# One decoder layer: all blocks projected first, three attentions and the routings moved beside the expert gathers

## What is computed

```python
h = x + W_o[ groupnorm(MLA heads) | groupnorm(FoX heads) ](rmsnorm(x))
y = h + PEER(rmsnorm(h))
# attention, 16 heads, causal over blocks of 128 queries:
s = q k^T * scale (+ c_q - c_k for the eight FoX heads); p = softmax(s + mask); o = p v
# PEER, per token and head (8 heads):
s = q . sub_keys (two sets of 128); top 16 of each; top 16 of the 256 sums; gate = softmax
act = gelu(peer_u[expert] . xb);  out = sum over 128 experts of (gate * act) * peer_v[expert]
```

## Time and profile before

| | us |
|---|---|
| median of the runs | 2458.63 |
| profiled execution, its own span, first to last instruction | 2563.8 |
| PE busy | 1793.9 (70%) |
| DVE busy | 1169.1 (46%) |
| POOL busy | 1190.8 (46%) |
| ACT busy | 348.5 (14%) |
| moved by DMA | 775.33 MB, mean 302 GB/s |
| first gather of peer_u issued | 513.3 |

### The profile page before, as it was taken

The page is one execution under the profiler, slowest core; times in us unless marked ns, Lnnn a source line. Parts: engine busy times, 40 slices in busy tenths (PEclk is TensorE's granted clock), DMA queues, the critical chain, the costliest instruction groups (busy, mean ns, idle before and its releaser), DMA issues.

```text
span 2563.8 us, 31875 instructions
## 1 busy us (share of the span) xinstructions
PE 1793.9 (70%) x11105; PEld 728.5 (28%) x11105; DVE 1169.1 (46%) x2804; ACT 348.5 (14%) x744; POOL 1190.8 (46%) x1076
## 2 busy tenths in 40 slices
PE   6788788855376999988399987631777523227878
PEld 1446445622232343333133332210111100001212
DVE  2334434499822702655680024765800155561352
ACT  1113213100011121322021212200000000000000
POOL 0000000046613656865665565688655444484673
PEclk9876888977689999999599997855899955557997
DMA  4000006069938999999999998999999999999995
GB/s 193 20 9 18 10 1 247 17 251 384 373 131 313 384 399 390 399 393 379 342 331 397 402 382 287 370 365 404 399 405 405 408 405 404 404 392 377 342 352 215
DMA packets 254251, 775.33 MB, mean 302 GB/s; under 512 B 36513, under 2 KB 45370, under 8 KB 250762
## 3 DMA queue, kind: packets, MB, share of 16 engines
q0 software_dynamic: 150784, 547.43, 55.3%
q1 hardware_dynamic: 102138, 221.64, 23.3%
q10 hardware_dynamic: 1168, 4.23, 0.4%
HBM read 766.36 MB, written 6.81 MB: 302 GB/s over the span
## 4 chain that ended last, share of the span: by engine, by line
PE 44%; DMA 24%; issue 12%; DVE 8%; POOL 5%; another core or an unknown queue 3%; ACT 2%; SPq 1%; DVEq 0%; POOLq 0%; ACTq 0%
DMA arena<-peer_v,idxT 14%; PE ps L1562 9%; PE ps L1624 9%; DMA arena<-peer_u,eidx 8%; PE ps L1368 7%; POOL arena L475 5%; PE ps L1610 3%; PE ps L1491 3%; PE ps L1640 2%; DVE arena L1176 2%; PE ps L1422 2%; DMA arena<-kpe_pool 2%; PE ps L1437 1%; PE ps L1412 1%
## 5 line engine op out<-in xcount | busy, mean ns | idle before, releaser
L475 POOL DMA_INDIRECT arena<-peer_u,eidx x512 | 622.2, 1215 | 872.5 <-DVE eidx L1086 512.8
L475 POOL DMA_INDIRECT arena<-peer_v,idxT x512 | 515.0, 1006 | 452.1 <-PE ps L1562 345.5
L1176 DVE CUSTOM_DVE_ANT_0 arena<-arena 128x1024 f32<-128x1024 f32 x384 | 467.0, 1226 | 529.9 <-DMA arena<-peer_u,eidx 457.7
L1562 PE MATMUL ps<-arena 128*32 128x512 f32 x2048 | 554.4, 632 | 125.9 <-DMA arena<-peer_v,idxT 112.5
L1624 PE MATMUL ps<-arena 128*128 128x512 f32 x512 | 303.4, 676 | 15.8 <-DMA arena<-kpe_pool 13.5
L1694 PE MATMUL ps<-arena 128*32 128x512 f32 x512 | 118.0, 874 | 236.5 <-DMA arena<-vn_pool 236.5
L1562 PEld LDWEIGHTS ps<-arena 128*32 128x32 f32 x2048 | 102.9, 111 | 441.0 <-DMA arena<-peer_v,idxT 321.1
L728 ACT ACTIVATE arena<-ps 128x512 f32<-128x512 f32 x256 | 150.0, 596 | 572.3 <-PE ps L1624 240.0
L1610 PE MATMUL ps<-arena 128*32 128x128 f32 x2048 | 177.1, 286 | 44.6 <-issue 35.6
L1368 PE MATMUL ps<-arena 128*128 128x512 f32 (+3 forms) x400 | 174.4, 597 | 6.9 <-DVE arena L952 6.6
L1176 DVE CUSTOM_DVE_ANT_0 arena<-arena,ps 128x1024 f32<-128x1024 f32 x128 | 151.4, 1219 | 11.4 <-DMA arena<-peer_u,eidx 5.3
(11 more groups left out here) (305 smaller groups left out, 1712.1 us busy)
## 6 DMA issues: line engine op xcount, KB each, us to landing
arena<-kt_pool SPq DMA_DIRECT2D x256, 320.0 KB
arena<-vn_pool SPq DMA_DIRECT2D x256, 320.0 KB
arena<-w_q SPq DMA_DIRECT2D x16, 1024.0 KB, 19.5
arena<-w_in SPq DMA_DIRECT2D x8, 1236.0 KB, 15.9
arena<-w_o SPq DMA_DIRECT2D x16, 512.0 KB, 6.9
arena<-peer_u,eidx POOLq DMA_INDIRECT x512
arena<-peer_v,idxT POOLq DMA_INDIRECT x512
arena<-kpe_pool SPq DMA_DIRECT2D x256, 16.0 KB
```

The costliest lines, as they stand in the source:

```text
L475: pool.indirect_dma_start(ring[:, q % RING, :], None, table, bass.IndirectOffsetOnAxis(ap=index, axis=0)).then_inc(g[q % RING], 16)
L1176: V_.tensor_tensor_reduce(rows, rows, x, 1.0, 0.0, ALU.mult, ALU.add, acc[:, k:k + 1]).then_inc(u_used, 1)
L1562: return T_.matmul(ps[32 * j:32 * j + 32, i, :], W32[:, j, c, :], ring[:, q % RING, 512 * i:512 * i + 512], start=(c == 0), stop=(c == 31) ...
```

## The change

All five tiles are projected before anything else runs on TensorE (`project_in(t, i, c)`), the head transposes of block t - 2 between the matmuls of tile t. The arena is laid out anew: each block has its own query tile, `w_in` lies where `w_o`, two quarters of `w_q` and the ring come later. Block 0's attention is done in groups of four heads between the last matmuls of block 3's projection; then come block 0's output projection and routing, with `w_q` in four quarters through two buffers. The whole of `w_q` is loaded a second time later.

The attention of blocks 1 (two heads a group), 2 and 3 (one head) runs while block 0's gathers arrive: TensorE runs it in one stream with the output projections of blocks 1 and 2 between the groups, and VectorE's maxima, mixtures and norms have fixed places between its dots (`beside_dots`). The causal mask is now added on TensorE, as a matmul of the identity with the mask, and all copies of transposed probabilities are ScalarE's. Block 0's dots read x from SBUF; the copy to PSUM is gone. Routing 1 is put between block 0's value matmuls, routings 2 and 3 into the time of block 1's dots. The cache units shift to later stages: 12 key units in the dots of block 1, 14 in its values, 38 in the dots of block 2; 24 value units in the values of block 2 and 40 in the dots of block 3.

```diff
-K_V0, K_U1, K_V1, K_U2 = range(0, 12), range(12, 36), range(36, 52), range(52, 64)
-V_U2, V_V2, V_U3 = range(0, 6), range(6, 16), range(16, NPG)
+K_U1, K_V1, K_U2 = range(0, 12), range(12, 26), range(26, 64)
+V_V2, V_U3 = range(0, 12), range(12, NPG)
+HPG = [4, 2, 1, 1]
+NG = [16 // m for m in HPG]
+GB = [sum(NG[:b]) for b in range(NB)]
...
+            sp.wait_ge(win_used, 1)
+            for c in range(4):
+                sp.dma_start(wo_ch[c], w_o[:, c, :]).then_inc(wo_in, 16)
+            load_wq_quarter(0)
+            sp.wait_ge(win_used, 4)
+            for c in range(4, DC):
+                sp.dma_start(wo_ch[c], w_o[:, c, :]).then_inc(wo_late_in, 16)
+            load_wq_quarter(1)
+            sp.wait_ge(o_ps, 4)
             sp.dma_start(hb[:, :], x_prompt[0:P, :]).then_inc(x_in, 16)
...
+            sp.wait_ge(q_ps, 1)
+            load_wq_quarter(2)
+            sp.wait_ge(q_ps, 2)
+            load_wq_quarter(3)
+            store_rows(4)
...
+            sp.wait_ge(o_ps, NGROUPS)
+            for c in (0, 1, 2, 3, 4, 5, 7):
+                sp.dma_start(wq[:, c, :], w_q[:, c, :]).then_inc(wq_in, 16)
+            sp.wait_ge(xn2_done, 3)
+            sp.wait_ge(h_stored[1], 16)
+            sp.wait_ge(h_stored[2], 16)
+            sp.dma_start(wq[:, 6, :], w_q[:, 6, :]).then_inc(wq_in, 16)
+            sp.wait_ge(op_ps, NB)
+            sp.dma_start(skT, sub_keys).then_inc(sk_late_in, 16)
...
+            def max_scores(b, gi):
+                G, w, m = GB[b] + gi, (b + 1) * P, HPG[b]
+                dve.wait_ge(s_ps, G + 1)
+                V_.tensor_reduce(nmx[:, m * gi:m * gi + m], heads(ps[:, s_bank(b, gi), 0:m * w], P, m), AX.X, ALU.max,
+                                 negate=True).then_inc(max_done, 1)
...
-                    x = ps[:, 0:2, :] if k >= IN_PS[b] else heads(xn2[:, b, :], P, 2)
+                    x = heads(xn2[:, b, :], P, 2)
...
+            beside_dots = {}
+
+            def at(k, f):
+                beside_dots.setdefault(k, []).append(f)
+
+            after_max = {2: {1: lambda: mixture(1), 2: mixture_mean, 3: lambda: mixture_scale(1),
+                             6: lambda: mixture_gain(1), 15: lambda: add_x(1)},
+                         3: {1: lambda: mixture(2), 2: mixture_mean, 3: lambda: mixture_scale(2),
+                             5: lambda: h_mean(1), 7: lambda: (norm2(1), mixture_gain(2)), 15: lambda: add_x(2)}}
+            for b in (2, 3):
+                for gi in range(16):
+                    k = 17 + gi + max(0, gi - 5) if b == 2 else 45 + 2 * gi
+                    at(k, lambda b=b, gi=gi: max_scores(b, gi))
+                    if gi in after_max[b]:
+                        at(k, after_max[b][gi])
+            at(78, lambda: mixture(3))
+            at(80, mixture_mean)
+            at(82, lambda: mixture_scale(3))
+            at(84, lambda: h_mean(2))
+            at(86, lambda: (norm2(2), mixture_gain(3)))
...
+            u_phase(0, beside_dots, 16, zero_W)
+
+            top_subkeys_of(1)
             top_experts(1)
             open_gates(1)
+            u_phase(1, {8: [lambda: add_y(0)], 40: [lambda: copy_idxT(1)], 48: [lambda: finish_gates(1)],
+                        72: [decode_queries_1], 80: [decode_queries_2], 88: [log_gate_rows]})
+            top_subkeys_of(2)
             top_experts(2)
             open_gates(2)
+            combine_chunk(0)
+            combine_chunk(1)
+            u_phase(2, {4: [lambda: decays(0)], 8: [lambda: add_y(1)], 16: [lambda: copy_idxT(2)],
+                        24: [lambda: combine_chunk(2)], 32: [lambda: finish_gates(2)], 40: [lambda: combine_chunk(3)],
+                        56: [lambda: decays(1), total_decay], 64: [lambda: combine_chunk(4)],
+                        90: [lambda: combine_chunk(5)], 114: [lambda: combine_chunk(6)]})
+            combine_chunk(7)
+            soften_1()
+            soften_2()
...
+            def scores(b, gi):
+                G, w = GB[b] + gi, (b + 1) * P
+                if b == 0 and gi:
+                    pe.wait_ge(exp_done, gi)
+                if b and G - 2 >= GB[1]:
+                    pe.wait_ge(exp_done, G - 1)
+                bank = s_bank(b, gi)
+                for j in range(HPG[b]):
+                    hh = HPG[b] * gi + j
                     kd = KM if hh < 8 else KF
+                    T_.matmul(ps[:, bank, j * w:(j + 1) * w], QT[b][0:kd, hh, :], KT[0:kd, hh, 0:w],
+                              start=True, stop=False, skip_group_check=True)
+                    last = T_.matmul(ps[:, bank, j * w + b * P:(j + 1) * w], ident, con[:, C_MASK:C_MASK + P],
+                                     start=False, stop=True, skip_group_check=True)
+                last.then_inc(s_ps, 1)
...
+            for t in (2, 3):
+                pe.wait_ge(fv_done, t)
+                for c in range(DC):
+                    project_in(t, 3, c)
+                pe.wait_ge(tail_read, t)
+                for c in range(DC):
+                    project_in(t, 2, c)
+                turn_heads(t - 2, range(0, 4))
+                for c in range(DC):
+                    project_in(t, 4, c)
+                turn_heads(t - 2, range(4, 8))
+                pe.wait_ge(head_read, t)
+                for c in range(DC):
+                    project_in(t, 0, c)
+                heads_turned(t - 2)
+                turn_x(t + 1)
+                turn_latents_in(t)
+                for c in range(DC):
+                    project_in(t, 1, c)
+                sum_decays(t - 1)
+                pe.wait_ge(xnT_done, t + 2)
+                expand_latents(t)
...
+            beside = [[lambda: scores(0, 0)],
+                      [lambda: turn(0, 0), lambda: scores(0, 1)],
...
+            for m in range(4 * 5):
+                c, i = 4 + m // 5, PROJ_ORDER[m % 5]
+                if m % 3 == 0 and m // 3 < len(beside):
+                    for f in beside[m // 3]:
+                        f()
+                last = project_in(NB, i, c)
+                if i == 1:
+                    if c < DC - 1:
+                        last.then_inc(win_used, 1)
+            turn_mixture(0)
+            project_out(0)
...
+            scores(1, 0)
+            order = [(b, gi) for b in range(1, NB) for gi in range(NG[b])]
+            for x, (b, gi) in enumerate(order):
+                if x + 1 < len(order):
+                    scores(*order[x + 1])
+                turn(b, gi)
+                if x:
+                    values(*order[x - 1])
+                if b > 1 and gi == 4:
+                    turn_mixture(b - 1)
+                if b > 1 and 7 <= gi < 15:
+                    project_out(b - 1, 2 * (gi - 7), 2 * (gi - 7) + 2)
+            values(*order[-1])
+            turn_mixture(3)
+            project_out(3)
...
-            v_phase(0, {16: turn_decode_queries, 24: absorb_decode_queries}, lambda k: step_beside(K_V0, 32, k))
-            turn_idx(1)
+            v_phase(0, {4: lambda: turn_rows(1), 12: lambda: query_rows(1, 0), 22: lambda: query_rows(1, 1),
+                        32: lambda: (turn_queries(1, 0), query_rows(1, 2)),
+                        43: lambda: (turn_queries(1, 1), subkey_scores(1, 0), query_rows(1, 3)),
+                        54: lambda: (turn_queries(1, 2), subkey_scores(1, 1)),
+                        58: lambda: (turn_queries(1, 3), subkey_scores(1, 2), subkey_scores(1, 3))})
+            for b in (2, 3):
+                turn_rows(b)
...
+                subkey_scores(b, 3)
+                if b == 2:
+                    turn_idx(1)
+            turn_decode_queries()
+            absorb_decode_queries()
+            pe.wait_ge(dq_done, 2)
             score_units(K_U1)
             turn_w(1)
-            v_phase(1, {}, lambda k: step_beside(K_V1, 0, k))
+            v_phase(1, {}, lambda k: step_beside(K_V1, 16, k))
             turn_idx(2)
             score_units(K_U2)
-            open_values()
-            value_units(V_U2)
             turn_w(2)
-            v_phase(2, {6 + 6 * i: lambda v=2 * V_V2[0] + i: value_unit(v) for i in range(2 * len(V_V2))})
+            values_at = {26 + 4 * i: lambda v=2 * V_V2[0] + i: value_unit(v) for i in range(2 * len(V_V2))}
+            v_phase(2, {20: open_values, **values_at})
```

1063 lines of the change are left out of this document (610 added, 453 removed).

## The result

| | kernel before | changed kernel | ratio |
|---|---|---|---|
| first comparison | 2459.39 us (2458.03 to 2470.38) | 2373.49 us (2369.24 to 2381.94) | 0.9643, 95% interval 0.9616 to 0.9669 |
| later, the third group of runs | 2461.84 | 2369.12 | 0.9627 (0.9604 to 0.9650) |
| later, the second group | 2561.45 | 2436.92 | 0.9527 (0.9425 to 0.9629) |

What follows compares the result with a forecast made beforehand. From 784 us transfers carry the kernel; the 513 us head and block 0's 271 us of dots can shrink. Values of block 0 at 600 plus 1756 for later stages make 2356, less 16 is 2340 us; range 2275 to 2405.

Steps and rivals of the forecast that it cites:

- (5): Values of block 1: 16 gathers alone 23 us, then 14 units 195; 218 us, 227 before.
- (7): Values of block 2: 26 gathers alone 37 us, 24 units 205, rest 8; 250 us, 234 before.
- Rival D: Head shrinks less, first gather at 400; dots of block 2 PE-bound at half clock, 425 us; about 2450 us, chance 0.05.
- (1): Head, up to the first gather: 325 us instead of 513, bounds 310 and 350.
- (2): Dots of block 0 with three attentions beside them: VectorE sets the stage, 273 us, values start at 600 for 784.
- Rival A: Half clock meets the attention beside block 0's dots: 50 us more, 2390 us in total, chance 0.13.
- (3): Values of block 0: 128 gathers at 1.49 us, routing 1 in PE's slack, covered by eight ring slots; 190 us for 221.
- (4): Dots of block 1: routings 2 and 3 first, then decode queries and 12 key units; 228 us, 279 before.
- (6): Dots of block 2: 38 key units instead of 12, PE's part 5.6 us a unit; 315 us, 288 before.
- (8): Dots of block 3: 40 value units for 32, 119.6 MB at 395 GB/s; 303 us, 279 before.
- Rival C: PE's 2 us gaps are the chip's and slow the attention beside block 0's dots; 2580 us, chance 0.08.
- Rival B: The 105 us between span and median are a uniform slowdown of the profiled execution; 2260 us, chance 0.09.

Runs made afterwards that it cites:

- att0_apart: Changed kernel with block 0's attention behind tile 4's projection matmuls instead of between them; first gather at 315 us, 22 us later than the changed kernel, same chip.
- after_third: The changed kernel, unedited, run again in the third group on a chip of the first kind: 2369.12 us, ratio to before 0.9627.
- v3: Changed kernel with routing 1 before block 0's values, 6 key units moved into block 2's values, value units 16 and 48: 2334.08 us, ratio to before 0.9487.
- r1_early: Changed kernel with all of block 1's routing ahead of block 0's value matmuls, on a second-kind chip: 2423.21 us, ratio to before 0.9453.
- half_norms: Changed kernel with each key unit's norm products over 256 of 512 columns (decode output wrong): 2357.5 us, dots of block 2 324 for 331.
- v2: Changed kernel with routing 1 early, routing 2 in half pieces among block 0's values, key units 16, 14, 34, decode queries earlier: 2436.44 us, changed kernel 2436.92.
- dots_quarter: Changed kernel with block 0's dots from the 17th on over 256 of 1024 columns (output wrong): that stage 247 us for 268.

## Why the prediction was right, and where its sum was off

**Right.** The stretch ahead of the first gather was the right one to shorten: on chips of the second kind it fell from 513 to 293 us, by 220, and the dots of block 0 took in three attentions for 10 us more (281 for 271), so the way to block 0's values fell by 210. The rest of the kernel gave 76 back, which leaves 134. That is also the main thing the prediction missed: it had the later seven stages at 1756 us against 1780, and they took 1856 on such a chip (1811 on the first kind). The total came within 34 us by luck, since errors went both ways: on the first kind -30 in the head, +54 in the later stages, +9 since the changed kernel's profile stands 7 us, not 16, above its median. Of its own signs the first gather (295, for 310 to 350) and the start of block 0's values (570, for 585 to 640) lie outside, and of the seven later stages only (5) and (7) came within 10 us.

Two of its sums are slips. Tiles 2 and 3 are "the same" as 40.5 plus 6.6 and 4, which makes 51 each and not 46, and a first gather near 335. Rival D adds 40 for dots of 2 at 425 us, where 425 less 315 is 110.

**(1) Head: 325 forecast, 295 and 293 measured.** The terms that failed are the additions per tile. From the first projection matmul of one to that of the next, tiles 2 and 3 took 39.8 and 40.0 us, not 46: 32 head transposes cost 3.8 us, not 6.6, and the "4 of longer sums and a wait on the copies" do not exist, as other matmuls stand there. That is 12 us; the tiles before them account for 5. Tile 4 with block 0's attention took 50, not 60 (46 to the last values, for 56): the attention had been priced at the 20 us that PE was busy at a granted clock of 0.57; between projection matmuls the clock stayed at 1.00 and of the 25.6 us that PE is busy in that stretch the projection has 15, which leaves the attention about 11. att0_apart shows that the place matters: apart, 22 us. The part behind it, 84 us, was forecast as 86.

**(2) Dots of block 0: 273 forecast (275 in the table), 274 (266 to 281 over all runs whose VectorE work there is the same).** To dot 16: 53 (54); to the last dot 215 (212); to the first value 6.8 (7). Waits on PE 25.5 (25). Rival A (half clock beside the dots, +50) did not happen: the clock was 0.60 up to dot 16, but 0.77 to 0.93 from there to the end of block 3's attention. POOL as the releaser of most dots did not either: it took 1.24 us a gather, not 1.57, and the releaser of its waits is the dots (70.4 us in after_third).

**(3) Values of 0: 190 forecast, 202.** Two errors that hid each other. "Eight ring slots cover a piece" failed: each piece of 7 to 8 us starves the ring. And 1.49 us per gather was too slow: with PE free, 128 gathers take 169 us (v3), 1.32 each, at 388 GB/s; on the second kind, where the earlier trace rows come from, 182 (r1_early), 1.42 each. The pieces cost 27 us (196 in after_third for 169), and PE stood idle 45 us just before that stage.

**(4) Dots of 1: 228 forecast, 246.** 92.4 MB went through in it (375 GB/s x 246.3 us), I had counted 84. SP issued 62 pages of keys in it, 15.5 units and not 12, since it fills the four slots ahead of the next stage, which is 4.8 MB; constants and weights of the decode part and two tiles of rows are about 2 MB more. 9 MB at 395 GB/s are 22 us.

**(6) Dots of 2: 315 forecast, 329 and 353.** Bytes as forecast (122.9 MB, 121.4 forecast). What failed is "PE's part of a unit 5.6 us, 213, below it": PE is busy 286 us in the stage, 7.5 a unit, and so behind when the gathers end. The last gather of block 2's dots is issued 45 us before the end of the stage, the last of the eight value gathers that fit into the ring 33 us before it; the key loads end 28 us before it. PE then works off the loaded units at 7.1 us each while nobody can issue more: 27.6 us x (1 - 233/400) = 12 us, nearly all of it in the last 13.6 us, at 67 GB/s. Making PE's share smaller shortened that tail (half_norms) and little else. On the second kind of chip the gaps come on top, 28 us of "issue" on PE. My rival D had PE bound this stage at the half clock; the clock was 0.95.

**(5), (7), (8), (9).** 221, 258, 314 and 241 for 218, 250, 303 and 252. On the second kind the last is 251, as the 252 of before. (7) and (8) run at 387 and 392 GB/s, where the earlier trace rows had 403 and 402. The loss is not spread over them; it lies in the first 72 us of (7) and the last 34 of (8), and between these the transfers run at 404 and 405:

```profile
1567.60:1640.00 72.40, 51.88 (x236) 11.41 (x236) 46.70 (x213) 4.82 (x6) 41.80 (x39) 0.82 0.91 343
1640.00:1826.00 186.00, 134.96 (x686) 30.79 (x690) 15.88 (x15) 3.18 (x12) 88.07 (x88) 0.93 1.03 404
1826.00:2106.00 280.00, 81.79 (x561) 23.76 (x553) 158.84 (x261) 4.79 (x18) 138.02 (x128) 0.52 1.03 405
2106.00:2139.50 33.50, 14.98 (x99) 4.20 (x99) 1.84 (x5) 3.15 (x4) 1.14 (x2) 0.50 0.75 291
```

That is 72.4 us x (1 - 343/404) = 11 and 33.5 x (1 - 291/405) = 9 us, for errors of 8 and 11. The second is the tail of the dots of 2 once more: POOL has filled the ring at 2107 and waits 33.5 us for PE. It was not varied by itself.

**The gaps.** "Such gaps are the profiled execution's own" was wrong: all three traces of the kernel before have them, each from a different comparison. Rival C (they are the chip's, and would ruin the attention beside the dots, 2580) was right on the owner, as far as the kinds can be told apart, and not on the price: the stage took 281 for 268 to 274. Rival B (uniform, 2260) fell. Taking them out was still right for the measured number, since that was taken on what looks like a chip of the other kind: good luck, not insight.

## What to carry to other kernels

Where two streams share the transfers, look at which of them ends first, and at what the other still has to do when nothing more can be issued; a unit moved from one stage to the next costs nearly the same there. A ring of slots that just keeps the transfers full has nothing left to cover a piece of other work on the engine that frees the slots: eight slots did not cover pieces of 7 to 8 us, and halves of them still cost 15 us in v2. An idle stretch of that engine just ahead is the better place. And before a gap in a profile is called noise, compare the profiled span with other times of the same chip, not with a median from elsewhere.

## What the runs showed of the hardware

- Two kinds of chip (or of state, see above), 2460 and 2565 us for one and the same program. In the slower, PE idles 1 to 2 us at a time without a releaser, in one stretch with the transfers at 379 GB/s, in another at 331. The cause stays open. PE's instruction packets give no sign of it: 16 KB, about 1.1 us each in either, and none falls between 598 and 640 us of the kernel before, where PE is busy 13.8 of 42 us.
- Block 0's attention behind the projection, its small matmuls waiting for each other, had a granted clock of 0.70, and 0.79 with the end of the projection; the same 144 records with the attention between the projection's matmuls had 1.00: 33.4 and 25.6 us.
- POOL's gather issue follows VectorE's two-SBUF-input work: 948 ns beside dots of 256 columns, 1210 beside dots of 1024, the same kind of gather in the same stretch (345 to 480 us).

```profile
L532 POOL DMA_INDIRECT arena<-peer_u,eidx x73 | 69.2, 948 | 67.6 <-DVE acc L1330 56.6 <-issue 11.0
```

```profile
L532 POOL DMA_INDIRECT arena<-peer_u,eidx x69 | 83.5, 1210 | 53.2 <-DVE acc L1329 39.8 <-issue 13.4
```

  These two rows (dots_quarter, after_third) agree with the Trainium skill, "SBUF — State Buffer", Who interferes with whom, by which VectorE and GpSimd share one pair of ports under an exclusive lock.
- SP needs 1.62 us per page whose address comes from a register, 7.1 us a key unit of 1.376 MB. By that, an estimate, one queue alone brings at most about 194 GB/s in this form.
